# A hybrid decoder step: page numbers are read ahead of the wait for the page's place, and VectorE's low halves and additions change order under w_o

## The chip, the cores and the metric

The kernel runs on one core of one Trainium2 chip. The core has five engines with a queue of instructions each, in order: TensorE (PE, with its weight loads listed apart as PEld), VectorE (DVE), ScalarE (ACT), GpSimd (POOL) and SyncE (SP). They meet only through semaphores. The metric is the device time of one execution in microseconds. An instruction that waits holds up all that stands behind it on its own queue.

## The reference

Two layers for 1024 new prompt tokens and 8 sampled tokens, all in float32; what the change touches lies in the first layer:

```
h      = rmsnorm(x, g)
q,k,v,f = split(h @ w_qkvf);  logf = log_sigmoid(f + b_f)
prompt: o = softmax(q k^T * 64**-0.5 + cum(logf)_q - cum(logf)_k, causal) v     # 16 heads of 64, 1024 rows
sample: ck, cv, clogf = cache[page_table]    # 8 sequences, 16 pages each, a page 128 rows x 16 heads x 64
        o = softmax(over 2048 cached rows and the new one) v
x = x + o @ w_o
x = x + swiglu(rmsnorm(x))                   # inner width 2816
```

The second layer has a short gated convolution in place of the attention, then the same swiglu; a final rmsnorm ends it. So the sampled tokens need 128 pages of keys and 128 pages of values, 512 KB each, whose places in the pool stand in page_table.

## The kernel before

T = 1032 columns (1024 prompt tokens and 8 samples) are held transposed, features on the 128 partitions, in 8 tiles of 128 features. Each matrix product in float32 is made of three passes with the operands split in a high and a low half (hi*hi, hi*lo, lo*hi): ScalarE makes the high halves by a copy to fp32r, GpSimd or VectorE the low halves by a subtraction. All engines' code is unrolled by hand, and tables of numbers (FILL, KEY_AT, VAL_AT) say in which of 15 slots of each of 8 head pairs a piece of work stands.

**Attention.** For each of the 8 pairs, TensorE makes scores, turns the probabilities, multiplies them with the values, and between these it projects the next pair's q, k and v (line 1836 to 1838). In the same slots the 128 key pages and 128 value pages of the samples go through. A key page: SP loads it to one of 3 places (`kpage`, KSLOT = 3), GpSimd multiplies it with the query (line 858, `multiply`), VectorE sums over the 64 numbers of each head (line 2351, `key_page`), and by that frees the place (semaphore `kfr`). A value page: SP loads it to one of 3 places (`vpage`, VSLOT = 3), TensorE multiplies it with the probabilities (line 1740, `page_product`) and frees the place (`vfr`). SP is one queue: loads of keys, of values, of weights and of the query stand in it in the order of the tables. `load_k` (line 580) and `load_v` (line 586) wait for the place, then read the page's number out of `pages_sb` in SBUF into a register (`page_id`, line 578), then start the transfer at that address.

**w_o.** The attention's output, 8 tiles of 128 features, is multiplied with w_o in two passes over the features: pass 0 takes tiles 0 and 1 for all 8 output tiles, pass 1 takes tiles 2 to 7 (`PASS`). Output tiles 0 and 1 of pass 0 are begun early (`prompt_steps`, line 1968), output tiles 2 to 7 follow (`out_pass`, line 1993). An output tile is accumulated in three PSUM banks of group i % 2 (`group`), so output tile 2 can only start when VectorE has taken tile 0 out of its group: `x_res = PS + x_old` (line 2802), which raises `ev`. The weights' halves come from ScalarE (`high`, line 1080) and GpSimd (`low`, line 831). The low halves of input tiles 2 to 7 are VectorE's (`out_low`, line 2635; it raises `blo`); they are read only in pass 1. `out_low(m)` waits for ScalarE's high half of tile m (line 1438, `bhi`). The place of tile 7's halves is that in which the raw tiles 2 and 3 lie, so they must have been read before. Then come the residual sums of pass 1 and the swiglu.

Of the kernel before, what the change touches and what calls it, by code (L numbers as in the profile page):

```python
# [44 lines left out]
def fox_shortconv_hybrid_step(  # L45
# [5 lines left out]
):  # L51

    _, S, D = x_prompt.shape
    NSEQ = x_sample.shape[0]
    _, POOL, PAGE, H, DH = cache_k.shape
    NPG = page_table.shape[1]
    DFF = w_ffn_out.shape[1]
    T = S + NSEQ
    KT = D // P
# [51 lines left out]
    k_pages = cache_k.rearrange("l g p h d -> (l g) p (h d)")  # L111
    v_pages = cache_v.rearrange("l g p h d -> (l g) p (h d)")
# [18 lines left out]
    with ctx:  # L131
# [3 lines left out]
        def sem(name):  # L135
            return ctx.enter_context(nc.semaphore(name))
# [4 lines left out]
        def group(s):  # L141

            return PS[:, 3 * s * BANK:3 * (s + 1) * BANK].rearrange("p (b n) -> p b n", b=NB)[:, :, 0:TB]
# [16 lines left out]
        def blocks(ap):  # L160
            return ap.rearrange("p (b n) -> p b n", b=NB)
# [136 lines left out]
        def bt(l, m):  # L298

            if m < 2:  # L300
                return b01[l][:, m, :], b01[l][:, 2 + m, :]
            if m < 6:
                return b25[:, m - 2, :], b25[:, 2 + m, :]
            return b67[m - 6][:, 0, :], b67[m - 6][:, 1, :]
# [176 lines left out]
        blo = sem("blo")  # L481
# [62 lines left out]
        def _(sp):  # L544
# [32 lines left out]
            def page_id(n):  # L577
                return sp.value_load(pages_sb[0:1, bass.ds(n, 1)], min_val=0, max_val=POOL - 1)

            def load_k(n):  # L580
                if n >= KSLOT:
                    sp.wait_ge(kfr, n - KSLOT + 1)
                src = k_pages[bass.ds(page_id(n), 1), :, :].rearrange("a p n -> p (a n)")
                sp.dma_start(kpage[:, n % KSLOT, :], src).then_inc(kin[n % KSLOT], 16)

            def load_v(n):
                m = NPROJ + n
                sp.wait_ge(vfr, m - VSLOT + 1)
                src = v_pages[bass.ds(page_id(n), 1), :, :].rearrange("a p n -> p (a n)")
                sp.dma_start(vpage[:, m % VSLOT, :], src).then_inc(vin[m % VSLOT], 16)  # L590

            def load_query(b):
# [21 lines left out]
            for g in range(KSLOT):  # L614
                load_k(g)
# [11 lines left out]
            for g in range(KSLOT, KSLOT + 3):  # L627
                load_k(g)
# [5 lines left out]
            for g in range(KSLOT + 3, KSLOT + FRONT_KEYS):  # L634
                load_k(g)
# [6 lines left out]
            def pair(i):  # L642
                for n in range(NSLOT):
# [37 lines left out]
                    for m in range(NPROJ + NPAGES - VSLOT):  # L681
                        if VAL_AT[m] == slot:
                            if m + VSLOT < NPROJ:
                                load_p(m + VSLOT)
                            else:
                                load_v(m + VSLOT - NPROJ)
# [379 lines left out]
        def _(act):  # L1066
# [9 lines left out]
            def high(s, kts=KT):  # L1076

                act.wait_ge(w_raw[s], wr[s].up())
                act.wait_ge(mm[s], done[s].up())
                act.activation(w_hi[s][:, 0:kts, :], raw[s][:, 0:kts, :], ACT.Copy).then_inc(w_hid[s], 1)  # L1080
# [350 lines left out]
            for m in range(2, KT + 2):  # L1431
                if m >= 4:
                    high(m % 2, 2)
                if m < KT:
                    act.wait_ge(oin[m % 4], 16 * (m // 4 + 1))
                    if m == 7:
                        act.wait_ge(blo, 4)
                    act.activation(bt(0, m)[0], o_st[m][:, 0:T], ACT.Copy).then_inc(bhi, 1)

            def final_rows():  # L1440
# [785 lines left out]
        def _(dve):  # L2226
# [163 lines left out]
            def maxima(i, n):  # L2390
                t, c = UNITS[n]
                _, w = unit_cols(n)
                for h in range(2):
                    dve.wait_ge(sd, 2 * (NUNIT * i + n) + h + 1)
                    ins = dve.tensor_reduce(nmax[:, t, h, c:c + 1], bank(h, 0, w), X_AXIS, ALU.max, negate=True)
                    if c == 0:
                        ins.then_inc(mxd, 1)
                if c == 1:
                    then(ins)
                    dve.tensor_reduce(nfin[:, 2 * t:2 * t + 2], nmax[:, t, :, :], X_AXIS, ALU.min).then_inc(mxd, 2)  # L2400
# [232 lines left out]
            def out_low(m):  # L2633
                dve.wait_ge(bhi, m + 2)
                dve.tensor_tensor(bt(0, m)[1], o_st[m][:, 0:T], bt(0, m)[0].bitcast(F32), ALU.subtract).then_inc(blo, 1)
# [157 lines left out]
                    reciprocals()  # L2793

            done0 = [done[s].value for s in range(2)]
            out_low(2)
            out_low(3)
            dve.wait_ge(xin, 16 * KT)
            for m in range(KT):
                s = m % 2  # L2800
                dve.wait_ge(mm[s], done[s].up())
                dve.tensor_tensor(blocks(x_res[:, m, :]), group(s), blocks(x_old[:, m, :]), ALU.add).then_inc(ev[s], 1)
                if m == 1:
                    for n in range(2):
                        dve.wait_ge(osp[n], 16 * 2 * NPAIR)
                if m + 4 < KT:
                    out_low(m + 4)
            bh.value = bl.value = B_TILES[0]
            sums_pass("ffn0")
            ffn(0, "mix1")  # L2810
# [75 lines left out]
```

## Time and profile before

| what | us |
|---|---|
| median of 3 runs (2650.67 to 2653.25) | 2650.95 |
| profiled execution | 2651.62 |
| its span, first to last instruction | 2649.9 |
| around the span | 1.7 |
| TensorE busy in the span | 2567.1 (97%) |
| attention as read here, 130 to 756 us of the span | 626 |
| first and last start of the value pages' transfers | 134.9, 744.0 |
| w_o, first output tile of line 1993 | starts at 763.4 |

The profile counts register instructions and waits as idle, so SP has no busy time of its own in it; its instructions appear as SPq. The chain of waits is followed back from the last instruction of the program: each piece was released by the one before it, so time that a piece of the chain loses is time of the whole, as long as no other chain is as long. TensorE's busy time contains the pipelined ends of its matmuls, so it is above what it computes.

### The profile page before, as it was taken

What the parts mean: (1) busy time and instruction counts of PE and PEld (TensorE: products, weight loads), DVE (VectorE), ACT (ScalarE), POOL (GpSimd) and SP (SyncE); (2) the same over time, 40 slices, a digit from 0 to 9 for tenths busy, and PEclk for the clock granted to TensorE, in tenths of its full rate; (3) what the DMA queues carried; (4) which work ended last, traced back from release to release, by engine and by line L of the source; (5) the groups of instructions that cost most, each with busy time, mean ns of one, the idle gap of its engine ahead of it and who ended that gap; (6) DMA issues with size and microseconds to landing.
All of it is one profiled execution on the core that took longest, in us unless ns stands there. A gap on an engine that the chain in (4) does not pass through costs nothing.

```text
span 2649.9 us, 45267 instructions
## 1 busy us (share of the span) xinstructions
PE 2567.1 (97%) x18462; PEld 2350.2 (89%) x18462; DVE 1657.3 (63%) x1948; ACT 967.3 (37%) x1838; POOL 1532.7 (58%) x871
## 2 busy tenths in 40 slices
PE   7899999999889999999999999999999999999999
PEld 5676666667579999999999999999989999999998
DVE  5676666766545666666666664444466666666665
ACT  4466665666645322222222231111432222222223
POOL 2766567666326866666666652212486666666661
PEclk9999999999999999999999999999999999999999
DMA  9776778777841211111111111111211112111112
GB/s 296 234 254 230 249 272 289 258 244 241 282 142 40 64 49 48 56 49 48 49 49 55 50 48 41 48 47 30 59 41 56 49 49 63 49 48 49 49 56 82
DMA packets 240573, 292.33 MB, mean 110 GB/s; under 512 B 12995, under 2 KB 193316, under 8 KB 240246
## 3 DMA queue, kind: packets, MB, share of 16 engines
q1 hardware_dynamic: 216658, 271.40, 31.8%
q10 hardware_dynamic: 23572, 17.12, 2.0%
q8 instruction: 139, 2.28, 0.3%
q0 software_dynamic: 144, 1.05, 0.1%
q14 instruction: 60, 0.49, 0.1%
HBM read 268.28 MB, written 21.28 MB: 109 GB/s over the span
## 4 chain that ended last, share of the span: by engine, by line
PE 78%; POOL 6%; DVE 5%; DMA 4%; issue 3%; ACT 2%; SPq 1%; DVEq 0%; ACTq 0%; POOLq 0%
PE PS L2065 32%; PE PS L1620 10%; PE PS L2157 6%; PE PS L2158 6%; PE PS L2156 6%; PE PS L1993 6%; POOL kpage L858 3%; PE PS L1836 2%; DMA vpage<-in_cache_v 2%; PE PS L1838 2%; PE PS L1837 2%; DMA kpage<-in_cache_k 1%; PE PS L1776 1%; DVE s_raw L2351 1%; PE PS L1740 1%
## 5 line engine op out<-in xcount | busy, mean ns | idle before, releaser
L831 POOL TENSOR_TENSOR w_lo<-raw,w_hi 128x1024 fp32r<-128x1024 f32 (+2 forms) x98 | 244.6, 2496 | 642.6 <-ACT w_hi L1525 281.6
L2065 PE MATMUL PS<-a_all,wb 128*128 128x258 f32 x3488 | 571.5, 284 | 5.3 <-POOL wb L991 3.6
L2065 PEld LDWEIGHTS PS<-a_all,wb 128*128 128x128 f32 x3488 | 486.4, 190 | 6.1 <-POOL wb L991 4.1
L2665 DVE TENSOR_TENSOR x_res<-PS,x_res 128x1032 f32<-128x1032 f32 (+2 forms) x400 | 399.6, 1016 | 74.6 <-PE PS L2158 64.8
L858 POOL TENSOR_TENSOR kpage<-kpage,q_bc 128x1024 f32<-128x1024 f32 x128 | 307.2, 2419 | 106.8 <-DMA kpage<-in_cache_k 85.8
L2065 PE MATMUL PS<-c_lo,wb 128*128 128x258 f32 x1744 | 352.5, 283 | 0.0
L2157 PE MATMUL PS<-wb,w_hi 128*128 128x344 f32 x960 | 308.0, 321 | 0.0
L2158 PE MATMUL PS<-wb,w_lo 128*128 128x344 f32 x960 | 307.8, 321 | 0.0
L2156 PE MATMUL PS<-wb,w_hi 128*128 128x344 f32 x960 | 305.7, 318 | 0.0
L2065 PEld LDWEIGHTS PS<-c_lo,wb 128*128 128x128 f32 x1744 | 271.8, 190 | 0.0
L1620 PE MATMUL PS<-a_all,w_hi 128*128 128x344 f32 x1152 | 213.4, 321 | 0.4 <-ACT rinv L1120 0.4
L2351 DVE TENSOR_REDUCE s_raw<-kpage 128x16 f32<-128x1024 f32 x128 | 153.7, 1210 | 60.7 <-POOL kpage L858 60.3
L1620 PEld LDWEIGHTS PS<-a_all,w_hi 128*128 128x128 f32 x1152 | 188.6, 188 | 0.8 <-ACT rinv L1120 0.4
L991 POOL TENSOR_TENSOR wb<-wbf,wb 128x512 fp32r<-128x512 f32 x126 | 165.3, 1312 | 40.5 <-ACT wb L1468 33.9
L2156 PEld LDWEIGHTS PS<-wb,w_hi 128*128 128x128 f32 x960 | 181.4, 189 | 0.0
L2158 PEld LDWEIGHTS PS<-wb,w_lo 128*128 128x128 f32 x960 | 180.6, 188 | 0.0
L2157 PEld LDWEIGHTS PS<-wb,w_hi 128*128 128x128 f32 x960 | 180.3, 188 | 0.0
L1468 ACT ACTIVATE wb<-wbf 128x512 fp32r<-128x512 f32 x130 | 81.5, 627 | 259.1 <-POOL wbf L995 258.2
L1836 PE MATMUL PS<-a_all,w_hi 128*128 128x512 f32 x384 | 173.5, 452 | 0.0
L1525 ACT ACTIVATE w_hi<-raw 128x1024 fp32r<-128x1024 f32 x42 | 44.6, 1063 | 305.9 <-PE PS L2158 305.9
L1018 POOL TENSOR_TENSOR wb<-f,wb 128x1032 fp32r<-128x1032 f32 x42 | 101.5, 2417 | 90.8 <-ACT wb L1512 90.8
L1838 PE MATMUL PS<-a_all,w_lo 128*128 128x512 f32 x384 | 153.2, 399 | 0.0
(352 smaller groups left out, 5482.5 us busy)
## 6 DMA issues: line engine op xcount, KB each, us to landing
kpage<-in_cache_k SPq DMA_DIRECT2D x128, 512.0 KB, 4.7
vpage<-in_cache_v SPq DMA_DIRECT2D x128, 512.0 KB, 5.1
raw<-in_w_ffn_in SPq DMA_DIRECT2D x88, 512.0 KB, 4.3
raw<-in_w_ffn_out SPq DMA_DIRECT2D x44, 512.0 KB, 3.5
raw<-in_attn_w_qkvf SPq DMA_DIRECT2D x24, 512.0 KB, 6.3
vpage<-in_attn_w_qkvf SPq DMA_DIRECT2D x24, 512.0 KB, 5.9
raw<-in_conv_w_in SPq DMA_DIRECT2D x24, 512.0 KB, 3.7
out<-raw ACTq DMA_DIRECT2D x16, 512.0 KB, 6.1
```

What stands on the lines that cost most here:

```text
L831: gp.tensor_tensor(w_lo[s][:, 0:kts, 0:cols], raw[s][:, 0:kts, 0:cols], w_hi[s][:, 0:kts, 0:cols].bitcast(F32), ALU.subtract).then_inc(w_l ...
L858: gp.tensor_tensor(kpage[:, n % KSLOT, :], kpage[:, n % KSLOT, :], q_bc[:, :], ALU.mult).then_inc(kml, 1)
L991: gp.tensor_tensor(lo, sum_ if x is None else x, hi.bitcast(F32), ALU.subtract).then_inc(wls, 1)
L1620: ins = pe.matmul(g[:, b, :], w[:, k, :], x[:, k, b * TB:(b + 1) * TB], start=k == 0 and n == 0, stop=k == KT - 1 and n == 2)
L1836: pe.matmul(bank(2 + a), w_hi[s][:, k, :], a_hi[:, k, x], start=k == 0, stop=False)
L1838: ins = pe.matmul(bank(2 + a), w_lo[s][:, k, :], a_hi[:, k, x], start=False, stop=k == KT - 1)
L2065: ins = pe.matmul(out[:, b, :], w[:, k, :], h[:, k, x, b * (HN // 2):(b + 1) * (HN // 2)], start=k == 0 and n == 0, stop=k == HK - 1 and n ...
L2156: pe.matmul(bank(n, 0, TB), hi[:, m, :], fb_hi[:, j % 2, x], start=True, stop=False)
L2157: pe.matmul(bank(n, 0, TB), hi[:, m, :], fb_lo[:, j % 2, x], start=False, stop=False)
L2158: ins = pe.matmul(bank(n, 0, TB), lo[:, m, :], fb_hi[:, j % 2, x], start=False, stop=True)
L2351: dve.tensor_reduce(s_raw[:, n % NPG, :], kpage[:, n % KSLOT, :].rearrange("p (h d) -> p h d", d=DH), X_AXIS, ALU.add).then_inc(kfr, 1)
L2665: ins = dve.tensor_tensor(x[:, at:at + n, :], src, x[:, at:at + n, :], ALU.add)
```

## The change

Two places. On SP, `load_k` and `load_v` read the page's number first and wait for the place after it. On VectorE, the addition of output tile 0 stands ahead of `out_low(2)`, that of output tile 1 ahead of `out_low(3)`, and so on; before, `out_low(2)` and `out_low(3)` stood ahead of both. Two waits go with it: VectorE waits for its own `out_low(3)` behind it, and ScalarE's copy of tile 7 waits for `blo` 5 and not 4.

```diff
             def load_k(n):
+                src = k_pages[bass.ds(page_id(n), 1), :, :].rearrange("a p n -> p (a n)")
                 if n >= KSLOT:
                     sp.wait_ge(kfr, n - KSLOT + 1)
-                src = k_pages[bass.ds(page_id(n), 1), :, :].rearrange("a p n -> p (a n)")
                 sp.dma_start(kpage[:, n % KSLOT, :], src).then_inc(kin[n % KSLOT], 16)

             def load_v(n):
                 m = NPROJ + n
+                src = v_pages[bass.ds(page_id(n), 1), :, :].rearrange("a p n -> p (a n)")
                 sp.wait_ge(vfr, m - VSLOT + 1)
-                src = v_pages[bass.ds(page_id(n), 1), :, :].rearrange("a p n -> p (a n)")
                 sp.dma_start(vpage[:, m % VSLOT, :], src).then_inc(vin[m % VSLOT], 16)
...
                     if m == 7:
-                        act.wait_ge(blo, 4)
+                        act.wait_ge(blo, 5)
...
-            out_low(2)
-            out_low(3)
             dve.wait_ge(xin, 16 * KT)
             for m in range(KT):
...
                 if m == 1:
                     for n in range(2):
                         dve.wait_ge(osp[n], 16 * 2 * NPAIR)
-                if m + 4 < KT:
-                    out_low(m + 4)
+                if m + 2 < KT:
+                    out_low(m + 2)
+                if m == 1:
+                    dve.wait_ge(blo, 5)
```

On SP, in the middle of the attention, one value page and one key page stand like this before (TENSOR_LOAD reads the number into a register, the ISA rows work out the address, DMA starts the transfer; `vfr` and `kfr` say that the place is free):

```order
L578 TENSOR_LOAD pages_sb [waits vfr]
L578 ISA x2
L590 ISA
L590 DMA vpage<-in_cache_v 128x1024
L578 TENSOR_LOAD pages_sb [waits kfr]
L578 ISA x2
L584 ISA
L584 DMA kpage<-in_cache_k 128x1024
```

and like this now:

```order
L578 TENSOR_LOAD pages_sb
L578 ISA x2
L590 ISA [waits vfr]
L590 DMA vpage<-in_cache_v 128x1024
L578 TENSOR_LOAD pages_sb
L578 ISA x2
L584 ISA [waits kfr]
L584 DMA kpage<-in_cache_k 128x1024
```

The wait moved from the register load to the last address instruction; the order of the transfers among each other is the same.

On VectorE, at the start of w_o, the piece of the difference is this (the rows of line 2635 are `out_low`, those of line 2800 or 2802 the additions, `mm0` and `mm1` say that TensorE has finished an output tile of group 0 or 1, `bhi` that ScalarE has made a high half, `osp` that the attention's output is stored):

```order
 L2628 TENSOR_TENSOR a_all<-o_smp,a_all 128x2x8 [waits blo,bhi]
-L2635 TENSOR_TENSOR wb<-a_f,wb 128x1032 [waits bhi,oas]
+L2800 TENSOR_TENSOR x_res<-PS,a_f 128x1032 [waits mm0,xin,oas]
 L2635 TENSOR_TENSOR wb<-a_f,wb 128x1032 [waits bhi]
-L2802 TENSOR_TENSOR x_res<-PS,a_f 128x1032 [waits mm0,xin]
+L2800 TENSOR_TENSOR x_res<-PS,a_f 128x1032 [waits mm1]
+L2635 TENSOR_TENSOR wb<-a_f,wb 128x1032 [waits bhi,osp1,osp0]
+L2800 TENSOR_TENSOR x_res<-PS,a_f 128x1032 [waits mm0,blo]
 L2635 TENSOR_TENSOR wb<-c_f,wb 128x1032 [waits bhi]
-L2802 TENSOR_TENSOR x_res<-PS,a_f 128x1032 [waits mm1]
-L2635 TENSOR_TENSOR wb<-c_f,wb 128x1032 [waits bhi,osp1,osp0]
-L2802 TENSOR_TENSOR x_res<-PS,a_f 128x1032 [waits mm0]
```

The first addition stood third and stands first; the number of instructions of each kind is the same.

## Rows read from the trace of the kernel before

**Rows 1.** Busy time by stage: the attention, and four stretches of it.

```profile
core 0: us, PE busy (x) PEld busy (x) DVE busy (x) ACT busy (x) POOL busy (x), PEclk, DMA share, GB/s
130.00:756.00 626.00, 589.34 (x4346) 421.79 (x4345) 411.64 (x743) 411.67 (x1058) 376.54 (x166) 0.97 0.75 255
240.00:250.00 10.00, 10.00 (x82) 7.61 (x84) 8.90 (x16) 7.30 (x19) 8.24 (x4) 1.00 0.56 187
210.00:220.00 10.00, 7.94 (x51) 5.28 (x52) 5.19 (x10) 4.47 (x14) 0.00 (x0) 0.83 1.02 384
580.00:590.00 10.00, 7.11 (x44) 5.04 (x43) 5.06 (x7) 3.30 (x6) 6.42 (x3) 0.72 0.97 336
```

**Rows 2.** Waits of SP's queue, 130 to 756 us: total us, times, longest.

```profile
SPq L578 <- DVE s_raw L2351: 194.4, 86, 11.0
SPq L578 <- PE PS L1740: 86.6, 48, 7.8
```

**Rows 3.** Waits of TensorE for value pages, and a short one of them.

```profile
PE PS L1740 <- DMA vpage<-in_cache_v: 19.4, 15, 2.9
...
453.50 0.61 PE L1740 MATMUL PS<-vpage,ps 128*4 128x256 f32 x8 [0.38 <-DMA vpage<-in_cache_v]
```

**Rows 4.** Chain of waits, a key page: start us, us, what.

```profile
491.38 1.13 DVE s_raw L2351
...
492.53 0.30 SPq L578
...
492.86 0.15 SPq L578
...
493.13 0.04 SPq L584
...
493.27 5.67 DMA kpage<-in_cache_k
```

**Rows 5.** Other page transfers on the chain, and a long read of a page's number.

```profile
156.14 3.53 DMA kpage<-in_cache_k
...
327.45 4.33 DMA kpage<-in_cache_k
...
446.24 1.13 SPq L578
...
506.84 5.12 DMA vpage<-in_cache_v
...
578.80 6.43 DMA vpage<-in_cache_v
...
742.90 5.43 DMA vpage<-in_cache_v
```

**Rows 6.** Order of time at the start of w_o: VectorE, GpSimd, ScalarE, TensorE.

```profile
759.63 0.32 PE L1968 MATMUL PS<-a_all,w_lo 128*128 128x344 f32 x1
759.63 2.38 DVE L2635 TENSOR_TENSOR wb<-a_f,wb 128x1032 fp32r<-128x1032 f32 x2 [1.13 <-ACT wb L1438]
760.39 0.40 ACT L1080 ACTIVATE w_hi<-raw 128x256 fp32r<-128x256 f32 x1
760.87 1.73 POOL L831 TENSOR_TENSOR w_lo<-raw,w_hi 128x256 fp32r<-128x256 f32 x1 [11.92 <-ACT w_hi L1080]
762.03 1.23 DVE L2802 TENSOR_TENSOR x_res<-PS,a_f 128x1032 f32<-128x1032 f32 x1
762.59 0.73 POOL L831 TENSOR_TENSOR w_lo<-raw,w_hi 128x256 fp32r<-128x256 f32 x1
763.41 1.18 PE L1993 MATMUL PS<-a_all,w_hi 128*128 128x344 f32 x6 [2.50 <-DVE x_res L2802]
```

**Rows 7.** Duration of line 2716, VectorE beside GpSimd: ns min/median/max.

```profile
L2716 DVE TENSOR_TENSOR f<-f x42: 1234/3309/3316, 886.3 to 2593.3; 128x1032 f32<-128x1032 f32 x42
```

**Rows 8.** Chain of waits behind the start of w_o.

```profile
763.41 14.43 PE PS L1993 x90
...
780.82 60.07 PE PS L1993 x378
```

## The prediction

> **What bounds the kernel now.** I read the busy time by stage first, then SP's and TensorE's waits, then the chain of waits through the attention, last the order of time around the start of w_o. In the attention (130 to 756 us) TensorE is busy 589 of 626 us and the DMA engines have a mean share of 0.75 [rows 1], so neither is idle for long, but they take turns. TensorE's largest wait there is for value pages: 19.4 us in 15 waits [rows 3]. SP waits at line 578, the read of a page's number, 86 times for a key place and 48 times for a value place [rows 2]; of the some 250 loads that wait for a place, more than half find SP standing there, and what SP does behind the wait is then paid after the place is free. In the chain the reader sees what that is: VectorE's reduction ends at 492.51, and the transfer starts at 493.27 [rows 4]. At the start of w_o TensorE stands still 2.50 us until VectorE's first addition is done [rows 6], and behind that the chain is TensorE for 14.43 us and, after 3 us of halves, for another 60.07 [rows 8].
>
> **Part one, the page number.** Behind the wait stand a register load, two address steps of line 578, two of line 584 and the DMA. After the change the first three stand ahead of it. From 492.53 to 493.13 they take 0.60 us with their gaps [rows 4]; with the commoner load of 0.27 us in place of 0.30 it is 0.57 us. Nothing is added: the same number of instructions, one wait moved. Where SP comes late and the place has long been free, the change does nothing, since the same instructions run in the same time.
>
> How often does it count? On the chain between 130 and 756 us 15 page transfers stand, the first at 156.14 and the last at 742.90 [rows 5]; 11 of them are started right after the place was freed, and 4 after the issue of another page that was itself released by a freed place. That is 15 crossings at 0.57 us = 8.6 us. In one of them, at 446.24, the register load took 1.13 us [rows 5], so there 1.43 us go, but TensorE waited only 0.38 us for that page [rows 3], so I count 0.38 and have 14 x 0.57 + 0.38 = 8.4 us as the upper end of what the chain can give directly.
>
> What speaks against the full sum is that a transfer which starts earlier need not land earlier. Three of the 15 land in 3.53 to 4.33 us; the other 12 take 5.12 to 6.43 [rows 5]. They lie in bursts where the DMA engines are 0.97 to 1.02 busy at 336 to 384 GB/s in the stretches 210 to 220 and 580 to 590 [rows 1], against 0.56 at 240 to 250, where one of the three short ones lies. In a burst the page stands behind others that are still being moved, and a start 0.57 us earlier mostly lengthens its own stay. The bounds of the 12 are therefore nothing and the full 0.57 us; no row shows where between them they lie. I take half: the bursts are full but not without gaps, and what was in the queue ahead was often started behind a moved wait too. So 3 x 0.57 = 1.7, 11 x 0.57 / 2 = 3.1, 0.38 / 2 = 0.2, together 5.0 us, with bounds of 1.7 and 8.4. A loss on the transfers themselves is excluded by the order: SP's loads follow each other as before.
>
> The Trainium skill, "DMA: Bandwidth & Descriptors", section "Latency and other measured facts", gives a floor of about 600 ns for a tensor_load; the trace has 0.27 to 0.30 us for the load alone and 1.13 us once, so by the page the saving would be an estimated 0.9 us a crossing, 13 us for 15, and the sum goes by the trace. The same skill, "SBUF — State Buffer", section "SBUF: two separate sides", puts HBM to one core at about 358 GB/s; the 336 to 384 GB/s of the bursts are at that ceiling, and this speaks against the change, since by it the 12 crossings in bursts would give nothing.
>
> **Part two, the order on VectorE.** Before, VectorE makes `out_low(2)` and `out_low(3)` from 759.63 to 762.01, then the addition until 763.26, and TensorE starts output tile 2 at 763.41 [rows 6]. The addition only needs TensorE's last matmul of output tile 0: it is the one that starts at 759.63 and takes 0.32, so it ends at 759.95 [rows 6]. Moved ahead, the addition can start at about 760.05 and ends 1.23 later, at 761.28, and TensorE could go on at 761.42. But output tile 2 also needs its weights' low half from GpSimd. That subtraction starts at 760.87, when ScalarE's high half is done, and took 1.73 us; the next one of the same size took 0.73 [rows 6]. The long one lay beside `out_low(3)`, which has two operands in SBUF, the short one beside the addition, which has one of them in PSUM. So beside the moved addition it should take 0.73 and end at 761.60. The second, `out_low(2)`, would come at 761.28, when GpSimd is at work, and VectorE would be the one that waits: line 2716, two SBUF operands as well, takes 1.23 us at its shortest and 3.31 as a rule [rows 7]. TensorE then starts at about 761.66 in place of 763.41: 1.75 us.
>
> The skill's rule ("SBUF — State Buffer", "SBUF: two separate sides") is that a VectorE instruction with two SBUF inputs and a GpSimd instruction exclude each other for a whole instruction, whoever came first; the 1.73 beside 0.73 agree with it. If `out_low(2)` came first instead, GpSimd would end at about 761.28 + 1.23 + 0.6 = 763.1, and TensorE would start at 763.2: only 0.2 us would be left, which I take as the lower end of this part.
>
> What is late next: output tile 3 needs the addition of tile 1. After the change `out_low(2)` runs from 761.60 to 762.83, the addition of tile 1 to 764.1, and TensorE reaches tile 3 at 761.66 + 2.9 = 764.5 (18 matmuls; 90 take 14.43 [rows 8]). It is ready 0.4 us early. GpSimd's next low half is held by `out_low(2)` from 762.59 to 762.83 and done by 763.6, also early. From there each output tile of 2.9 us has one addition and one `out_low` of together 2.5 us on VectorE. The last low half is done at about 776, and pass 1, which reads it, starts at about 779. The added waits cost nothing: `blo` 5 is reached at about 765.4, some 2 us before ScalarE comes to tile 7, and what VectorE's own wait holds up is the addition of tile 2, needed at 767.4 and done by 766.7. The stores that `osp` stands for were done when SP began its last load of them, before 760. TensorE's 14.43 and 60.07 us behind this start move as a block, so I take 1.7 us, bounds 0.2 and 1.8.
>
> **Sum.** 5.0 + 1.7 = 6.7 us. The profiled execution took 2651.62 us (span 2649.9 and 1.7 around it), so 2644.9; it lies 0.7 above the median of 2650.95, so as a median 2644.3. Of the 5.0 I expect that other waits (TensorE for VectorE's output sums, ScalarE's exponentials) take a little back, and put the prediction at 2644.5.
>
> **Rivals.**
>
> 1. The transfers are at their ceiling: in the bursts nothing lands earlier, and only the three crossings outside them count, 1.7 us. With part two at 0.2 to 1.7 this is 1.9 to 3.4, so 2647.5 to 2649. For it: the share of 0.97 to 1.02 [rows 1]. Against it: the stage's mean share is 0.75, so even within bursts there are gaps that an earlier start could fill. That the read ahead does nothing because SP is never early is the end of this case; the 134 waits [rows 2] speak against it.
>
> 2. The chain gives all it has: 8.4 + 1.7 = 10.1 us, 2640.9. For it: TensorE's 15 waits are longer than 0.57 us on the mean (19.4 / 15 = 1.3 us [rows 3]), and 281 us of SP's waits show that the queue is early. Against it: rival 1, and that another chain is as long in some places.
>
> 3. The clock: after TensorE's long waits its granted clock falls; 580 to 590, where TensorE is busy 7.11 of 10 us, has a mean of 0.72 of the 2.4 GHz level, and the whole attention has 0.97 [rows 1]. Each hundredth of that mean is 6.3 us of the 626. Were the waits to fall so that the mean is 0.95, 12.5 us would be lost against 6.7 gained, 2656.8, slower. It decides from 0.96 on. For it: the fall is tied to where waits lie, and the change moves all of them. Against it: they become shorter, which should rather raise the clock.
>
> **How the numbers follow.** The forecast has 0.48, rival 1 has 0.32, rival 2 has 0.13, rival 3 has 0.07. What a measurement of this kernel can tell from no change is about 0.2%, 5.3 us. The forecast's own range, with a quarter to three quarters of the 12 crossings, is 4.8 to 8.4 us, so nine tenths of it, 0.43, lie beyond 5.3 us; with rival 2 that makes 0.56 for faster. Rival 1 and the rest of the forecast make 0.37 for no change, and 0.07 is slower. The range reaches from the upper end of rival 2 to most of rival 1: 2640 to 2649.5; left out are rival 3, the end of rival 1 and some of rival 2.
>
> **What would show it.** In the profile after, between the end of a releaser and a page's transfer in the chain there should be 0.2 us and not 0.75, and SP's waits should stand at lines 584 and 590 (with their new numbers) and no longer at 578. TensorE's waits for value pages should be near 19.4 - 5 us; if they stay at 19 while the transfers' time to landing grows by 0.5 us, it is rival 1. At w_o, GpSimd's first low half should take 0.73 us, and TensorE's first matmul of line 1993 should follow the last of line 1968 after 0.8 us in place of 2.5. From the start of w_o to the end the two traces should agree within 1 us. The prediction is wrong if the attention is not at least 2 us shorter, or if what w_o's start gains is given back by the start of pass 1.

## The result and the profile after

The changed kernel takes 2638.12 us in the median of 5 runs (2636.41 to 2638.42), the kernel before 2652.74 on the same chip. The ratio is 0.9942 with a 95% interval of 0.9927 to 0.9956, so 15.4 us less, between 11.7 and 19.4. Measured again with the experiments, it came to 0.9945 (0.9931 to 0.9958). That is more than twice the 6.7 us forecast, beyond the range (2640.0 to 2649.5), and more than rival 2 gave (2640.9), which came nearest. The sign was right.

The two profiled executions, 2651.62 and 2636.41 us, are cut at four places of equal work: the split of the first head pair's keys (line 1174), line 2628 at the end of the attention, the first matmul of pass 1, the end. First the kernel before: stretch, width, busy time of each engine with its instructions, granted clock, DMA share, GB/s.

```profile
0.00:82.83 82.83, 65.76 (x394) 43.36 (x395) 49.28 (x68) 34.95 (x52) 31.15 (x36) 0.96 0.87 284
82.83:758.33 675.50, 632.38 (x4589) 453.38 (x4589) 441.50 (x792) 433.89 (x1111) 413.56 (x184) 0.97 0.74 252
758.33:780.82 22.49, 19.84 (x126) 19.29 (x124) 15.86 (x17) 9.26 (x14) 7.34 (x8) 1.00 0.45 152
780.82:2649.90 1869.08, 1849.11 (x13358) 1834.14 (x13358) 1150.65 (x1075) 489.19 (x663) 1080.66 (x644) 1.00 0.17 51
```

The same stretches of the changed kernel:

```profile
0.00:80.79 80.79, 62.37 (x394) 41.62 (x395) 49.31 (x68) 34.84 (x52) 31.51 (x36) 1.00 0.90 291
80.79:744.64 663.85, 623.53 (x4589) 449.36 (x4589) 441.19 (x793) 433.99 (x1111) 413.48 (x184) 0.98 0.75 257
744.64:766.07 21.43, 20.13 (x126) 19.28 (x124) 15.93 (x17) 9.26 (x14) 7.19 (x8) 1.00 0.47 160
766.07:2634.70 1868.63, 1844.71 (x13358) 1831.59 (x13358) 1152.01 (x1075) 489.08 (x663) 1081.25 (x644) 1.00 0.17 51
```

The attention is 11.65 us shorter, the start of w_o 1.06, and the rest agrees to 0.45. The first stretch has 2.04 us in it that the change can't have made, since its instructions are the same: the clock was 0.96 in one and 1.00 in the other. Executions of one kernel differ by some us in the attention too: the same stretch takes 668.0 us in b_only, whose attention is that of the kernel before, and 668.5 in after_again, the changed kernel once more (both below). So the 11.65 shows little by itself; what each part is worth is taken from the timed runs below, and the traces say where.

SP's waits have moved to the lines of the transfers. First the changed kernel's waits of SP's queue over the stretch that answers to 130 to 756 us, then TensorE's (total us, times, longest):

```profile
SPq L584 <- DVE s_raw L2351: 186.4, 84, 11.3
SPq L590 <- PE PS L1740: 78.3, 43, 7.6
```

```profile
PE PS L1740 <- DMA vpage<-in_cache_v: 17.0, 13, 1.8
```

Against [rows 2] SP stands there 16.3 us less, 127 times in place of 134. TensorE's waits for value pages fell from 19.4 [rows 3] to 17.0 only, the longest from 2.9 to 1.8 us. The larger fall is GpSimd's wait for key pages, from 85.8 to 72.8 us, a row that the prediction did not read; the experiments below show it and use it as a gauge. In the chain, a key page now reads thus (compare [rows 4]):

```profile
484.51 1.13 DVE s_raw L2351
...
485.66 0.04 SPq L584
...
485.74 0.03 SPq L584
...
485.80 5.27 DMA kpage<-in_cache_k
```

The reduction ends at 485.64 and the transfer starts at 485.80: 0.16 us in place of 0.76. Over the whole attention, SP's steps of the page loads (lines 578 to 590) are 109 rows with 13.3 us of the chain before, from 83.06 to 742.84, and 57 rows with 5.1 us after, from 81.01 to 730.96. The 8.2 us between are close to the prediction's upper end for the chain, 8.4. Whether the pages also landed earlier, other rows tell. The page issues of the attention, KB each and median us to landing, before and after:

```profile
kpage<-in_cache_k SPq DMA_DIRECT2D x125, 512.0 KB, 4.7
vpage<-in_cache_v SPq DMA_DIRECT2D x128, 512.0 KB, 5.1
```

```profile
kpage<-in_cache_k SPq DMA_DIRECT2D x125, 512.0 KB, 4.8
vpage<-in_cache_v SPq DMA_DIRECT2D x128, 512.0 KB, 5.3
```

The medians grew by 0.1 to 0.2 us, but they mix pages that SP stood waiting for with pages that it came late to, whose start the change does not move. Worked out page by page from the traces, for the pages that SP waited for, this is the mean time in us from the freed place to the landing (number of pages in brackets). The last two columns are those of them in whose first 5 us the DMA engines had a share of 0.9 or more, so the bursts. b_only has the attention of the kernel before, a_only and after_again that of the changed one.

| run | keys | values | keys in bursts | values in bursts |
|---|---|---|---|---|
| before | 5.25 (96) | 5.40 (49) | 5.92 (41) | 6.00 (24) |
| b_only | 5.24 (95) | 5.37 (44) | 5.80 (39) | 6.05 (21) |
| a_only | 4.69 (96) | 4.83 (41) | 5.40 (38) | 5.44 (16) |
| after | 4.71 (93) | 4.86 (44) | 5.47 (35) | 5.41 (20) |
| after_again | 4.67 (92) | 4.93 (43) | 5.39 (40) | 5.50 (20) |

The start behind the freed place is some 0.6 us earlier; about 0.5 of it arrives, and in bursts 0.3 to 0.6.

The start of w_o in the changed kernel, in order of time (idle time before an instruction in brackets, with its releaser):

```profile
746.39 1.23 DVE L2800 TENSOR_TENSOR x_res<-PS,a_f 128x1032 f32<-128x1032 f32 x1 [1.58 <-PE PS L1968]
746.69 0.40 ACT L1080 ACTIVATE w_hi<-raw 128x256 fp32r<-128x256 f32 x1
747.16 0.73 POOL L831 TENSOR_TENSOR w_lo<-raw,w_hi 128x256 fp32r<-128x256 f32 x1 [9.49 <-ACT w_hi L1080]
747.54 1.44 DVE L2635 TENSOR_TENSOR wb<-a_f,wb 128x1032 fp32r<-128x1032 f32 x1
747.95 1.21 PE L1993 MATMUL PS<-a_all,w_hi 128*128 128x344 f32 x6 [0.73 <-POOL w_lo L831]
...
752.18 0.42 ACT L1080 ACTIVATE w_hi<-raw 128x256 fp32r<-128x256 f32 x1 [2.18 <-DMA raw<-in_attn_w_o]
752.45 1.22 DVE L2635 TENSOR_TENSOR wb<-c_f,wb 128x1032 fp32r<-128x1032 f32 x1
752.68 1.58 POOL L831 TENSOR_TENSOR w_lo<-raw,w_hi 128x256 fp32r<-128x256 f32 x1 [2.92 <-ACT w_hi L1080]
754.31 1.21 PE L1993 MATMUL PS<-a_all,w_hi 128*128 128x344 f32 x6 [0.42 <-POOL w_lo L831]
```

Up to 747.95 this is the order worked out in the prediction: the addition first, GpSimd's low half in 0.73 us beside it, `out_low(2)` held up by GpSimd (it starts 0.35 us before that low half ends and takes 1.44, the next one 1.22), TensorE on after 0.73 us in place of 2.50. Counted from line 2628, output tile 2 starts at 3.31 us and not at 5.08, 1.77 earlier; 1.75 was forecast. Then 0.7 of it are given back, at a place that the prediction passed over ("from there each output tile ..."). Output tile 4 is the first whose weights are loaded into a buffer freed in w_o; its low half comes to lie beside `out_low(4)` and takes 1.58 us, and TensorE waits 0.42. In the traces of the other four runs with this order TensorE waits 0.42 to 0.78 us at this place; the longest is b_only's, where the low half takes 0.74 us and the weights are late, by a landing of 5.40 us in place of 4.19.

### The profile page after: what moved, and what is told of

Same layout as the page of the kernel before. It is cut to its first block, busy times and chain, and to the rows that moved or that the text cites. A ratio compares the mean times of both kernels' runs of the same rounds, so it can differ in the third digit from the quotient of the medians.

```text
span 2634.7 us, 45267 instructions
## 1 busy us (share of the span) xinstructions
PE 2550.7 (97%) x18462; PEld 2341.8 (89%) x18462; DVE 1658.4 (63%) x1948; ACT 967.2 (37%) x1838; POOL 1533.4 (58%) x871
## 4 chain that ended last, share of the span: by engine, by line
PE 79%; POOL 6%; DVE 5%; DMA 4%; ACT 3%; issue 3%; SPq 0%; ACTq 0%; DVEq 0%; POOLq 0%
PE PS L2065 32%; PE PS L1620 10%; PE PS L2157 6%; PE PS L2158 6%; PE PS L2156 6%; PE PS L1993 5%; POOL kpage L858 3%; PE PS L1836 2%; PE PS L1837 2%; PE PS L1838 2%; DMA kpage<-in_cache_k 2%; PE PS L1776 1%; DMA vpage<-in_cache_v 1%; DVE s_raw L2351 1%; PE PS L1740 1%
## 5 line engine op out<-in xcount | busy, mean ns | idle before, releaser
L858 POOL TENSOR_TENSOR kpage<-kpage,q_bc 128x1024 f32<-128x1024 f32 x128 | 307.1, 2418 | 93.2 <-DMA kpage<-in_cache_k 72.8
```

What stands on the lines that cost most here:

```text
L858: gp.tensor_tensor(kpage[:, n % KSLOT, :], kpage[:, n % KSLOT, :], q_bc[:, :], ALU.mult).then_inc(kml, 1)
```

## The experiments

Fifteen runs, each timed beside the kernel before on the same chip. The last column is us against before, worked out from the ratio and 2652 us:

| run | what is in it | ratio (95%) | us |
|---|---|---|---|
| a_only | part one alone | 0.9960 (0.9945 to 0.9975) | -10.6 |
| b_only | part two alone | 0.9994 (0.9984 to 1.0003) | -1.6 |
| keys_only | part one, keys alone | 0.9967 (0.9955 to 0.9979) | -8.8 |
| vals_only | part one, values alone | 0.9986 (0.9977 to 0.9995) | -3.7 |
| read_twice | before, two reads behind the wait | 1.0091 (1.0076 to 1.0105) | +24.1 |
| ahead_behind | one read ahead, one behind | 1.0046 (1.0034 to 1.0058) | +12.2 |
| ahead_twice | two reads ahead | 1.0012 (1.0003 to 1.0021) | +3.2 |
| slot_ahead | after, a slot's reads together | 0.9965 (0.9953 to 0.9976) | -9.3 |
| read_once | after, one read for key and value | 0.9956 (0.9942 to 0.9970) | -11.7 |
| fill | before, small matmuls ahead of 6 pages | 0.9992 (0.9981 to 1.0002) | -2.1 |
| after_again | the changed kernel | 0.9945 (0.9931 to 0.9958) | -14.6 |
| half_before, half_ahead | values halved by partitions | 1.0032, 0.9996 | +8.5, -1.1 |
| cols_before, cols_ahead | values halved by columns | 0.9913, 0.9894 | -23.1, -28.1 |

**The parts apart.** The edit of a_only is the diff's first hunk alone, that of b_only the other two.

> Only the page numbers are read ahead of the wait, keys and values; VectorE's order as before. Theory 1 (the read ahead is worth more than the chain's crossings at half, since shorter waits of TensorE also mean fewer falls of its clock): 11 to 14 us below the kernel before, 0.9950 of it, and TensorE's idle time between the first key copy and the end of attention falls by about 3 us while its busy time falls by 6 to 9. Theory 2 (the prediction's sum was right and the rest of the 15 us is chance in where the clock falls, the 2 us before any moved wait among it): about 5 us, 0.9980. Theory 3 (the two parts only work together): under 3 us.

> Only VectorE's order at the start of w_o is changed. From the two traces: output tile 2 of w_o starts 1.77 us earlier, and 0.7 us of it is given back before pass 1, since the weights of output tile 4 are loaded behind GpSimd's low half of tile 2 and come late; so 1.1 us below the kernel before, 0.9996. Theory 3 (only together) would need much more than that or a loss here.

Part one has most of it: 10.6 us, with an interval of 6.6 to 14.6 that leaves out theory 2's 5. Theory 1's sign, TensorE's busy time, is no evidence: over the attention it is 626.3 us in a_only and 632.4 before, but 626.0 in b_only too, where the attention is that of the kernel before. Its idle time there is 38.3 us, against 43.1 and 42.0. Part two alone can't be told from nothing by its time. The two add up to -12.2, the whole measured -14.6 and -15.4; the intervals hold both.

**Keys and values apart.** In keys_only `load_k` alone is changed, in vals_only `load_v` alone.

> Only key pages read their number ahead. Of the 15 crossings on the chain of before, 10 stand behind a freed key place (6 key transfers and 4 value transfers issued right after a key's). Theory 1a (the chain of keys, GpSimd and VectorE is what counts): two thirds of the whole, 8 us. Theory 1b (TensorE's waits for value pages are what counts, and a key that starts earlier only stands ahead of a value in the queue): under 4 us.

> Only value pages read their number ahead. Of the 15 crossings 5 stand behind a freed value place. Theory 1a: a third of the whole, 4 us. Theory 1b: 8 us or more. If both this and keys_only give most of the 12, the gains are not additive and one wait hides the other.

Some two thirds come from the keys by the two ratios, whose intervals (5.6 to 11.9 and 1.3 to 6.1 us) overlap a little. GpSimd's wait for key pages, 85.8 us before, is 76.4 in keys_only and 83.2 in vals_only. What vals_only gained does not show in TensorE's wait for value pages, which is 20.2 us there and 19.4 before.

**What a read behind the wait costs.**

```
 load_k, load_v of before:
     wait_ge(...)
+    page_id(n)
     src = ...page_id(n)...
```

> The kernel before with each page's number read twice behind the wait, so about 0.57 us more between a freed place and its transfer; nothing else. Theory 1 (each us of latency behind the wait is paid in full, at 134 waits and on more than one chain): as far above the kernel before as a_only lies below it, 9 to 12 us, 1.004. Theory 2 (the DMA engines are at their ceiling in the bursts, and the gain of a_only was the clock's doing): under 4 us, since a later start meets a queue that is still full. More than 15 us would mean that the waits add up faster than they can be taken away.

A second 0.57 us behind each wait costs 24 us, more than double what taking the first away gave. So the bursts don't swallow a delay. But it is two things at once, latency behind the wait and SP's time for each page. The next two runs separate them, with two reads each:

```
 ahead_behind:  src = ...page_id(n)...; wait_ge(...); page_id(n)
 ahead_twice:   page_id(n); src = ...page_id(n)...; wait_ge(...)
```

> The kernel before with two reads of each page number, one ahead of the wait for the page's place and one behind it. Only what stands behind a wait matters (theory 1, latency): one read is behind it, as in the kernel before, so -3 to +5 us against before. Both matter (theory 2): of the +24 us of the kernel that reads twice behind the wait, 10.6 are the second read behind it, as the first one was worth that, and the other 13 are SyncE being late with two reads for each page; those 13 are paid here, so +8 to +18 us. Only SyncE's time per page matters (theory 3): +20 to +28 us, as with both behind the wait.

> The kernel before with two reads of each page number, both ahead of the wait. Theory 1 (latency alone): as with one read ahead, -7 to -13 us against before. Theory 2 (latency and SyncE's lateness): -10.6 + 13 = about +3 us, -3 to +8. Theory 3 (SyncE's time per page alone): +20 to +28 us, as much as the kernel with one read on either side.

Theory 2 foretold +13 and +3; measured were +12.2 and +3.2. Moving one read from behind the wait to ahead of it gives 10.6 (before to a_only), 11.9 (read_twice to ahead_behind) and 9.0 us (ahead_behind to ahead_twice). An added read costs 13.8 us (a_only to ahead_twice) and 12.2 (before to ahead_behind) where the number behind stays the same. The count of SP's waits for a freed place goes with it: 144 before and 137 in a_only, but 89, 79 and 75 in read_twice, ahead_behind and ahead_twice, so with two reads SP comes late to more pages. GpSimd's multiplications of keys show the same steps: busy us, mean ns, then idle time before them and what ended it, for before, a_only, read_twice, ahead_behind and ahead_twice:

```profile
L858 POOL TENSOR_TENSOR kpage<-kpage,q_bc 128x1024 f32<-128x1024 f32 x126 | 301.5, 2412 | 100.2 <-DMA kpage<-in_cache_k 85.8 <-DMA q_bc<-q_spill 14.0
```

```profile
L858 POOL TENSOR_TENSOR kpage<-kpage,q_bc 128x1024 f32<-128x1024 f32 x126 | 301.2, 2406 | 90.0 <-DMA kpage<-in_cache_k 75.7 <-DMA q_bc<-q_spill 14.0
```

```profile
L860 POOL TENSOR_TENSOR kpage<-kpage,q_bc 128x1024 f32<-128x1024 f32 x126 | 301.5, 2407 | 125.8 <-DMA kpage<-in_cache_k 106.9 <-DMA q_bc<-q_spill 18.3
```

```profile
L860 POOL TENSOR_TENSOR kpage<-kpage,q_bc 128x1024 f32<-128x1024 f32 x126 | 299.2, 2390 | 114.5 <-DMA kpage<-in_cache_k 97.4 <-DMA q_bc<-q_spill 16.7
```

```profile
L860 POOL TENSOR_TENSOR kpage<-kpage,q_bc 128x1024 f32<-128x1024 f32 x126 | 301.3, 2409 | 103.5 <-DMA kpage<-in_cache_k 87.0 <-DMA q_bc<-q_spill 16.4
```

The wait for key pages is 85.8, 75.7, 106.9, 97.4, 87.0 us: moving a read ahead takes 10.1, 9.5 and 10.4 us off it, adding one puts 11.3 to 11.6 on, about what the time does. In the changed kernel it is 72.8, here by the row of the whole execution:

```profile
L858 POOL TENSOR_TENSOR kpage<-kpage,q_bc 128x1024 f32<-128x1024 f32 x128 | 307.1, 2418 | 93.2 <-DMA kpage<-in_cache_k 72.8
```

One trace is good to some 3 us: with the same loads it is 75.7 in a_only and 75.4 in after_again, and with those of before 82.3 in b_only.

**Further ahead, and fewer reads.** In slot_ahead all numbers of a slot are read before its first wait. In read_once the key's load keeps its number in a register for the value's load:

```
 load_k:  + numbers[n] = page_id(n)
 load_v:  - src = v_pages[bass.ds(page_id(n), 1), ...
          + src = v_pages[bass.ds(numbers.pop(n), 1), ...
```

> The changed kernel (both parts), with the numbers of all pages of a slot read before the slot's first wait, so that a value page behind a key page starts 0.57 us earlier still. In the changed kernel's chain 4 value transfers stand right behind a key's issue. Theory 1: 2 to 4 us below the changed kernel. If the queue of transfers is the limit: the same as the changed kernel.

> The changed kernel with each page number read once: the value's load takes the register that the key's load read (up to 21 are held), so SyncE has 119 reads fewer in attention. Theory 2 (each read costs SyncE's time as well, +12 to +14 us for a second read of all pages ahead of the wait): half of the reads go, so about 6 us less than the changed kernel, -18 to -23 us against before. Theory 1 (only what stands behind a wait matters): as the changed kernel, -12 to -17 us.

Neither is faster than the changed kernel. In slot_ahead TensorE's waits for value pages are 21.1 us, 17.0 in the changed kernel. One reading is that the first page of a slot stands behind the reads of the others, a delay where SP is late. But SP waits for a place 159 times there, 136 times in the changed kernel, and value pages land in 5.8 us by the median in place of 5.3, so it may be what read_once shows next; no run separates the two. In read_once theory 2 fails downwards: less time of SP for each page gave nothing. Its trace (an execution of 2636.72 us, the fastest of five) shows where the time may have gone. The waits of SP's queue, 80 to 757 us, in read_once:

```profile
SPq L587 <- DVE s_raw L2354: 248.2, 101, 11.4
SPq L593 <- PE PS L1743: 117.7, 57, 8.0
```

and the median time to landing there:

```profile
vpage<-in_cache_v SPq DMA_DIRECT2D x128, 512.0 KB, 5.9
kpage<-in_cache_k SPq DMA_DIRECT2D x125, 512.0 KB, 4.8
```

SP is early more often, 158 waits with 366 us against 136 with 282 in the changed kernel's attention, but the value pages stay 5.9 us in the queue in place of 5.3. GpSimd's wait for keys is 72.9 us against 72.8, TensorE's for values 16.2 against 17.0. For the pages that SP waited for, freed place to landing is 5.17 us for values and 4.82 for keys, against 4.86 and 4.71. This would be rival 1, one step further on: the transfers swallow the earlier start. It rests on one trace, and no run tests it.

**Less traffic.** The value transfers are halved, with the number read behind and ahead of the wait; first by partitions, then by columns:

```
 half:  vpage[0:64, slot, :]   <- src[0:64, :]
 cols:  vpage[:, slot, 0:D//2] <- src[:, 0:D//2]
```

> The kernel before, the value pages' transfers cut to the first 64 of 128 partitions (the other half of each place keeps old numbers, so the output is not the reference's). It is the base of the next run. If the transfers' length is what the chain pays (theory 1), value pages land over 2 us sooner and TensorE's 19.4 us of waits for them go to under 8: -8 to -20 us against before, and SyncE's waits for places move to the keys. If the ceiling of the DMA engines isn't in play at all, -3 to +3.

> The same halved value transfers, with every page number read ahead of the wait. The prediction's step, that transfers in bursts swallow half of an earlier start: with a quarter of the pages' bytes gone less is swallowed and the read ahead gives more than with full traffic, 12 to 16 us against the run with halved transfers and the number behind the wait. The theory that bursts swallow little and the gain is an earlier landing of pages that come just in time: value pages aren't late any more, the keys' part is left, 5 to 9 us against that run.

The cut by partitions is no test of the ceiling: half of the bytes landed in 4.7 us (median) against 5.1, and the kernel became 8.5 us slower, for which I have no cause; the traced execution, with 2652.54 us the fastest of six, can't show one. Reading ahead gave 9.5 us in it all the same (0.9996 / 1.0032 = 0.9964), between the two theories.

> The kernel before, the value pages' transfers cut to the first 512 of 1024 columns in all 128 partitions (the other columns of each place keep old numbers, so the output is not the reference's). The cut by partitions left the median landing at 4.7 us against 5.1; if here it goes to 3 us or so, TensorE's waits for value pages (19.4 us) go to under 10 and the time falls by 5 to 20 us. If the landing again stays above 4.5 us, -3 to +8 us, and the next run is no test of bursts either.

> The same cut by columns, with every page number read ahead of the wait; against the run with the same cut and the number behind the wait. The prediction's step (bursts swallow half of an earlier start): with less traffic less is swallowed, 12 to 16 us gained. The theory that bursts swallow little: the keys' part stays and the values' part shrinks as their pages are less often late, 6 to 11 us gained.

By columns the landing did fall. The page issues of cols_before and the wait of TensorE there:

```profile
kpage<-in_cache_k SPq DMA_DIRECT2D x125, 512.0 KB, 4.2
vpage<-in_cache_v SPq DMA_DIRECT2D x128, 256.0 KB, 3.6
```

```profile
PE PS L1740 <- DMA vpage<-in_cache_v: 7.6, 9, 1.7
```

With half of the value pages' traffic gone, reading ahead gives 0.9894 / 0.9913 = 0.9981 (0.9960 to 1.0002, from the two half widths of 0.0016 and 0.0014 as the root of their squares), 5.1 us, at most 10.6. The prediction's step wanted more than with full traffic, 12 to 16, and that is outside: the gain does not sit behind a ceiling that less traffic would lift. That it is smaller than with full traffic is not shown, since 10.6 there has an interval of 6.6 to 14.6, and the waits fall by as much here: GpSimd's for key pages from 76.3 to 67.1 us, TensorE's for value pages from 7.6 to 3.4. My own 6 to 11 lies above the 5.1, and the interval holds most of it.

**The clock.** In six places where TensorE waits long for a value page, twelve small matmuls on a spare bank were put ahead of the wait, so that it isn't idle there:

```
+ if b * NPG + g in (14, 55, 71, 87, 103, 126):
+     for _ in range(12): pe.matmul(bank(7, 416, 512), ident_b[:, :], mask_b[:, 0:96], ...)
  pe.wait_ge(vin[n % VSLOT], ...)
```

> The kernel before with 12 small matmuls on TensorE ahead of its wait for six value pages (numbers 14, 55, 71, 87, 103, 126, where it waited 1.5 to 2.9 us); they go to columns of PSUM that nothing else uses. They cost about 1.2 us each only where TensorE doesn't wait. Theory of the clock (the granted clock falls to 1.2 GHz behind such waits, and a fall costs about 1.7 us of TensorE's work): five falls fewer, up to 8 us below the kernel before. If the falls behind these waits cost nothing, because other waits absorb them: the same as before, or up to 3 us above.

The stage and one of its stretches, which had clocks of 0.97 and 0.72 before [rows 1]:

```profile
130.00:756.00 626.00, 585.97 (x4432) 418.72 (x4431) 413.28 (x754) 411.06 (x1058) 376.00 (x166) 0.99 0.75 255
580.00:590.00 10.00, 8.29 (x77) 5.77 (x75) 7.51 (x12) 6.42 (x15) 7.77 (x5) 1.00 0.94 336
```

Twelve of these matmuls take 0.68 us where they run at once, not the 1.2 expected. In the trace before, the clock fell behind the wait at five of the six places; in this one it is 1.00 behind all six. The stage's clock rose by two hundredths, which by rival 3's price of 6.3 us each would be 12.5; the time fell by 2.1, with an interval that reaches to no gain at all. Part of what TensorE did faster came back as waiting; its wait for value pages there:

```profile
PE PS L1744 <- DMA vpage<-in_cache_v: 22.9, 18, 2.7
```

It was 19.4 in 15 [rows 3]. So the rise from 0.97 to 0.98 in the changed kernel explains little of its gain: two hundredths gave at most 5.0 us here, so one gives an estimated 2.5 at most.

**The whole again.**

> The changed kernel once more, on the same chip as the three others. From its two parts alone (10.6 and 1.6 us) 12 us below the kernel before; if its first 15 us were partly chance in the clock of the front, where nothing is changed, it should come out at 10 to 13; at 15 again the two parts are worth more together.

It agrees with the first measurement.

## Why the prediction was wrong

- **The step that failed** is in part one: "I take half", the 11 crossings in bursts at 3.1 us in place of 6.3. From a DMA share of 0.97 to 1.02 [rows 1] I took it that a page started earlier stays longer. It does, but by less than half: by the table above, in bursts 0.3 to 0.6 of the 0.6 us arrive, about as much as for all pages. So the term belonged nearer to its upper bound, 6.3, and part one nearer to 8.4. The timed runs agree: part one measured 10.6 us, between 6.6 and 14.6, with 8.4 inside and 5.0 not; moving a read past the wait is worth the same 9 to 12 us from three bases; and less traffic did not make it worth more. The rule of about 358 GB/s ("SBUF — State Buffer" in the Trainium skill, section "SBUF: two separate sides") was weighed as speaking for rival 1. The traces do not show such a ceiling: stretches of 384 [rows 1] and 393 GB/s (a_only, below) lie above it.
- **What was not counted in part one**: only TensorE's 19.4 us of waits for values were read as what could shrink. The larger wait that the reads feed is GpSimd's for key pages, 85.8 us, and some two thirds of the gain came by the keys. The start of the count at 130 us left nothing out: the two key pages of the chain ahead of it, at 83.94 and 97.00, stand behind weight loads that SP waits with, and they start 1.27 and 1.38 us after these, before and after alike. The forecast's own range, 4.8 to 8.4, comes out of its terms as 5.1 to 8.4.
- **What was right in it**: the crossing (0.16 us against "0.2 and not 0.75"), the lines at which SP waits, that nothing is lost where SP is late. "TensorE's waits for value pages should be near 19.4 - 5" came true in a_only (14.9) and not in the changed kernel (17.0, and 16.8 in after_again); rival 1 did not hold all the same, because landing did not grow by 0.5.
- **Part two** had its mechanism and its first number right, 1.77 us against 1.75. What is kept by the start of pass 1 is 1.06 in the pair of traces, since output tile 4 gives 0.7 back; alone it measured 1.6, between 4.2 less and 0.8 more than before.
- **What part two left out is the clock.** Of the kernel before, one trace was read, and in it the clock stays at 1.00 behind the wait of 2.50 us. In a_only the same wait, to 754.21, is followed by a fall:

```profile
754.21 1.18 PE L1993 MATMUL PS<-a_all,w_hi 128*128 128x344 f32 x6 [2.50 <-DVE x_res L2802]
```

  The stretches of 3 us there (clock, DMA share and GB/s are the last three):

```profile
751.00:754.00 3.00, 0.71 (x5) 0.42 (x3) 2.97 (x4) 2.70 (x5) 2.34 (x2) 1.00 1.00 393
754.00:757.00 3.00, 2.79 (x13) 2.82 (x14) 3.00 (x4) 0.20 (x1) 0.07 (x1) 0.74 0.71 257
757.00:760.00 3.00, 3.00 (x15) 3.00 (x15) 1.72 (x2) 1.21 (x2) 0.71 (x1) 0.69 0.00 0
```

  0.74 and 0.69 over 3 us each are 1.7 us of TensorE at a place where the chain is TensorE. The traces of all runs together show how often. Twelve of them have the old order: in five the clock stays, and from line 2628 to pass 1 it is 22.5 us; in seven it falls (fill and cols_before, with the number behind the wait, among them), and it is 24.0. The five with the new order, b_only among them, wait 0.73 us, have a clock of 1.00 behind it, and take 21.4 to 21.8. So part two is worth 0.7 to 1.1 us in an execution in which the clock would have stayed, and 2.2 to 2.6 in one in which it would have fallen.
- **Rival 3** is out: the clock of the attention did not fall, and fill shows that it weighs less there than I priced it.
- **Open**: the chain's upper end (8.4 us) and part two (0.7 to 2.6) make 9.1 to 11.0, and the whole measured 14.6 and 15.4, with intervals that begin at 11.1 and 11.7. After_again less a_only is 4.0 us, an uncertain number from two chips. Chance, waits off the chain that was followed and fewer falls of the clock in the attention are candidates for the rest; none is shown.

## What to carry to other kernels

Where a queue waits for a buffer, everything between the wait and the transfer is paid on every page that comes just in time, so put reads and address steps ahead of the wait, and judge it by the consumer's waits (here GpSimd's for keys) in more than one trace, not by the share of the DMA engines in a burst. A busy burst isn't a ceiling until the time to landing grows by as much as the start came earlier: read that, for the pages that the queue waited for. Here ahead of one wait was enough; more ahead (slot_ahead) or less work in a queue that is already early (read_once) gave nothing more. And where an order of instructions leaves TensorE a wait, one trace may not show what the clock does behind it: look at several.

## What the hardware showed that was not expected

- A cut of a page's transfer from 128 to 64 partitions halves the bytes and leaves the median landing at 4.7 us against 5.1, with the stage's DMA share at 0.70 against 0.74; a cut of its columns by half lands in 3.6 us.
- The same wait of 2.50 us before output tile 2 was followed by full clock in five executions and by a fall in seven, which costs 1.5 us up to pass 1 (24.0 in place of 22.5); a wait of 0.73 us was followed by none in five.
- Six places of the attention had a clock of 1.00 behind twelve small matmuls each, five of which had a fall before, and the time fell by 2.1 us, at most 5.0.
